# Expert gathers of a PEER block: second choice and first Gelu moved, V rows and dense V spread differently

## What is computed

```python
q = (hf @ w_q).reshape(n_tok, 8, 2, 128)                       # 8 heads, two half queries
half_scores = einsum('thpd,hpnd->thpn', q, sub_keys)           # 128 keys in each half
s_top, i_top = top_k(half_scores, 16)
cand = s_top[:, :, 0, :, None] + s_top[:, :, 1, None, :]       # 16 x 16 pairs
best, pos = top_k(cand, 16); expert_idx = take(i0 * 128 + i1, pos); gates = softmax(best)
act = einsum('td,thkd->thk', xb, u_tab[ib])                    # 16384 experts, rows of 2048
w = gates * gelu(act)
out = einsum('thk,thkd->td', w, v_tab[ib])
x = layer_norm(alpha * x + (1 + gate2) * out)
```

## Time and profile before

| | us |
|---|---|
| median of 3 runs (2278.86 to 2285.75) | 2281.61 |
| the profiled execution, its own time | 2278.52 |
| its span, from first to last instruction | 2276.9 |
| PE busy, share of the span | 1937.7, 85% |
| DVE busy | 1365.1, 60% |
| POOL busy | 782.8, 34% |
| ACT busy | 390.6, 17% |
| all of DMA: 722.41 MB, mean | 317 GB/s |

### The profile page before, as it was taken

How to read it: one execution, slowest core, us unless ns; L and a number is a source line. 1 busy time by engine, 2 the same in 40 slices (tenths; PEclk the granted TensorE clock), 3 DMA queues, 4 the chain that set the end, 5 groups by cost and what they waited for, 6 DMA issues and landing times.

```text
span 2276.9 us, 27806 instructions
## 1 busy us (share of the span) xinstructions
PE 1937.7 (85%) x10646; PEld 1309.3 (58%) x10646; DVE 1365.1 (60%) x2008; ACT 390.6 (17%) x1001; POOL 782.8 (34%) x554
## 2 busy tenths in 40 slices
PE   4899899998999999989888888888975888897455
PEld 4788688887888888878654545555640222221001
DVE  7821378776444441246798889777876444444664
ACT  0112212211000001021232212544530000000011
POOL 1000000000000000004365546767878644554783
PEclk9999899999999999999899899888985999999556
DMA  9963366575576656318899999999999999999997
GB/s 391 428 276 143 116 270 246 216 292 197 234 284 245 230 212 259 140 69 331 311 383 414 405 408 414 398 402 398 392 406 371 417 417 410 399 413 354 364 365 270
DMA packets 104603, 722.41 MB, mean 317 GB/s; under 512 B 29740, under 2 KB 29740, under 8 KB 32060
## 3 DMA queue, kind: packets, MB, share of 16 engines
q0 software_dynamic: 78800, 466.66, 51.9%
q1 hardware_dynamic: 25696, 254.35, 28.0%
HBM read 858.35 MB, written 4.19 MB: 379 GB/s over the span
## 4 chain that ended last, share of the span: by engine, by line
PE 43%; DMA 29%; DVE 12%; issue 8%; POOL 5%; ACT 2%; POOLq 0%; DVEq 0%; SPq 0%; ACTq 0%
PE ps L777 21%; DMA arena<-expert_u,expert 14%; DMA arena<-expert_v,expert_q 11%; PE ps L785 10%; POOL arena L489 4%; PE ps L801 3%; PE ps L974 3%; DVE work L1410 2%; PE ps L1002 2%; DMA mod_rows<-expert_u,expert 2%; DVE mod_rows L1167 1%; PE ps L1048 1%; DMA mod_rows<-expert_v,expert_q 1%; DVE work L1223 1%; DVE work L1130 1%
## 5 line engine op out<-in xcount | busy, mean ns | idle before, releaser
L1410 DVE CUSTOM_DVE_ANT_0 work<-arena,buf_b 128x2048 f32<-128x2048 f32 x166 | 380.8, 2294 | 265.5 <-DMA arena<-expert_u,expert 232.1
L974 PE MATMUL ps<-arena,mod_rows 128*32 128x512 f32 x1640 | 270.5, 740 | 197.1 <-DMA arena<-expert_v,expert_q 166.0
L777 PE MATMUL ps<-buf_a,arena 128*128 128x256 f32 x1920 | 424.2, 383 | 6.1 <-DVE arena L1241 5.3
L777 PEld LDWEIGHTS ps<-buf_a,arena 128*128 128x128 f32 x1920 | 367.5, 192 | 57.2 <-issue 6.7
L489 POOL DMA_INDIRECT arena<-expert_v,expert_q x205 | 339.8, 1658 | 159.1 <-PE ps L974 97.1
L489 POOL DMA_INDIRECT arena<-expert_u,expert x205 | 266.1, 1298 | 239.8 <-DVE work L1410 124.2
L476 POOL DMA_DIRECT2D arena<-ada_late x32 | 16.9, 529 | 770.9 <-DVE mod_rows L1167 642.7
L1002 PE MATMUL ps<-arena 128*128 128x256 f32 x1024 | 273.3, 418 | 4.2 <-DMA arena<-dense_u 4.2
L1002 PEld LDWEIGHTS ps<-arena 128*128 128x128 f32 x1024 | 202.8, 207 | 128.8 <-issue 94.8
L974 PEld LDWEIGHTS ps<-arena,mod_rows 128*32 128x32 f32 x1640 | 37.2, 118 | 333.2 <-DMA arena<-expert_v,expert_q 270.3
L653 ACT ACTIVATE work<-work 32x4 f32<-32x4 f32 (+3 forms) x320 | 66.4, 207 | 551.3 <-DVE work L1410 543.8
(11 more groups left out here) (244 smaller groups left out, 2083.1 us busy)
## 6 DMA issues: line engine op xcount, KB each, us to landing
arena<-weights SPq DMA_DIRECT2D x62, 2048.0 KB, 8.0
arena<-ada_late POOLq DMA_DIRECT2D x32, 2048.0 KB, 9.4
arena<-ada_early SPq DMA_DIRECT2D x16, 2048.0 KB, 17.7
arena<-dense_u SPq DMA_DIRECT2D x32, 1024.0 KB
arena<-expert_v SPq DMA_DIRECT2D x32, 1024.0 KB
arena<-w_early SPq DMA_DIRECT2D x8, 1536.0 KB, 9.8
arena<-expert_u,expert POOLq DMA_INDIRECT x205
arena<-expert_v,expert_q POOLq DMA_INDIRECT x205
```

The costliest lines, as they stand in the source:

```text
L777: last = mm(ps[:, bank, c * TOKENS:(c + 1) * TOKENS], ring[slot][:, first + k, c * P:(c + 1) * P], rhs[:, k, :], start=(k == 0), stop=(k = ...
L974: last = mm(ps[j * GROUP:(j + 1) * GROUP, n // HEADS * QUADS + g, :], spread_w[n % 2][:, e, :], v_slot[row % V_RING][:, j * QCOLS:(j + 1) ...
L1410: v.tensor_tensor_reduce(out=products[n > 2], in0=u_slot[s], in1=h2[:, n // HEADS], scale=1.0, scalar=0.0, op0=ALU.mult, op1=ALU.add, accu ...
```

## The change

It moves work within the fixed orders of the PEER stage; no operation is added or left out in what is computed.

- The second choice is made beside the rows (0, 1), (0, 3), (0, 5), (0, 7).
- ACT: `soft_exp(1)` stands at projection 3, and `gates_to_quads(0)` with `gelu(0)` at projection 5 (all three stood at projection 4).
- PE: the last two projections are cut into eight groups of matmuls each, with a V row of head 0 after each, so all 16 V(0) rows are done there. The loop for n = 1 then has no V rows.
- POOL: V(0, 5) to V(0, 15) are issued beside U(1, 4) to U(1, 10), one or two to a step.
- The pieces of the first 20 dense U tiles are spread over (1, 0) to (4, 15) (before: (1, 9) to (4, 15)). `GELU_AT` follows from it.
- The pieces of dense V are spread over the 81 steps (9, 13) to (14, 13) (before: the 64 steps (10, 0) to (13, 15)).
- Block 0's rows are added from (15, 4) on, every second row, and finished behind the last U row; means, variances and rstd move accordingly, and two table preloads of ACT in head 15 go.

```diff
@@ -355,17 +355,18 @@
         F_END = tuple(n + m * 4 for n, m in zip(F_QUERY, (1, 1, 0, 0)))
 
         FIRST_MASKS = 5
-        FIRST_BESIDE = 8
         row_order = [(n, e) for n in range(BLOCKS * HEADS) for e in range(TOPK)]
-        choice_steps = row_order[2:TOPK:4] + [row_order[TOPK + i * 64 // 56] for i in range(56)]
-        dense_steps = [row_order[TOPK + FIRST_BESIDE + 1:5 * TOPK], row_order[5 * TOPK:9 * TOPK - 4]]
+        choice_steps = row_order[1:TOPK // 2:2] + [row_order[TOPK + i * 64 // 56] for i in range(56)]
+        dense_steps = [row_order[TOPK:5 * TOPK], row_order[5 * TOPK:9 * TOPK - 4]]
         mask_steps = [(n, e) for n in range(FIRST_MASKS, HEADS + 1) for e in range(TOPK)]
-        v_steps = [(n, e) for n in range(HEADS + 2, HEADS + 6) for e in range(TOPK)]
+        v_steps = row_order[10 * TOPK - 3:15 * TOPK - 2]
 
         def shares(steps, count):
 
             return {step: range(i * count // len(steps), (i + 1) * count // len(steps)) for i, step in enumerate(steps)}
 
+        LATER_V0 = {e: range(V_RING + first, V_RING + end) for e, first, end in
+                    ((4, 0, 2), (5, 2, 3), (6, 3, 5), (7, 5, 6), (8, 6, 8), (9, 8, 9), (10, 9, 11))}
         BEFORE_MASKS = 20
         DENSE_U_AT = shares(dense_steps[0], 4 * BEFORE_MASKS)
         for step, pieces in shares(dense_steps[1], 4 * (DENSE - BEFORE_MASKS)).items():
@@ -517,8 +518,9 @@
                         wait_alone(pool, s_exq, (2, 5, HEADS + 1).index(n) + 2)
                     if n > 1:
                         gather_v(n - 1, e)
-                    elif V_RING <= e + 1 < TOPK:
-                        gather_v(0, e + 1)
+                    else:
+                        for later in LATER_V0.get(e, ()):
+                            gather_v(0, later)
             for e in range(TOPK):
                 gather_v(BLOCKS * HEADS - 1, e)
 
@@ -732,8 +734,9 @@
                     soft_exp(0)
                 if h == 1:
                     experts_to_quads(0)
-                if h == 4:
+                if h == 3:
                     soft_exp(1)
+                if h == 5:
                     gates_to_quads(0)
                     gelu(0)
                 if h == 6:
@@ -755,12 +758,9 @@
                     for t in TOKENS_AT.get((n, e), ()):
                         if t % 2 == 0:
                             mask_cols(t)
-                    if n == BLOCKS * HEADS - 1 and e == 6:
-                        nc.scalar.preload_act_table_set("natural_log_exp_and_others")
-                        rstd_of_groups(0, 0, QUADS)
-                        nc.scalar.preload_act_table_set("gelu_and_others")
                 gelu(n)
             nc.scalar.preload_act_table_set("natural_log_exp_and_others")
+            rstd_of_groups(0, 0, QUADS)
             for g in range(QUADS):
                 rstd_of_groups(1 + g, QUADS + g, QUADS + g + 1)
 
@@ -1043,16 +1043,16 @@
             for h in range(HEADS):
                 s = h % 2
                 pe.wait_ge(loaded[s], (F_QUERY[s] + h // 2 + 1) * 16)
-                for i in range(4):
-                    for k in range(8 * (i % 2), 8 * (i % 2) + 8):
-                        last = mm(ps[:, 6 + s, i // 2 * TOKENS:(i // 2 + 1) * TOKENS], ring[s][:, k, i // 2 * P:(i // 2 + 1) * P],
+                for i in range(8):
+                    for k in range(4 * (i % 4), 4 * (i % 4) + 4):
+                        last = mm(ps[:, 6 + s, i // 4 * TOKENS:(i // 4 + 1) * TOKENS], ring[s][:, k, i // 4 * P:(i // 4 + 1) * P],
                                   h2_t[:, k, :], start=k == 0, stop=k == KT - 1)
-                    if i == 3:
+                    if i == 7:
                         last.then_inc(used[s], 1)
                     if h == HEADS - 2 and i == 0:
                         pe.wait_ge(s_wgt, 1)
                     if h >= HEADS - 2:
-                        weigh_row(0, 4 * (h - HEADS + 2) + i)
+                        weigh_row(0, 8 * (h - HEADS + 2) + i)
                 pe.wait_ge(s_pq, h + 1)
                 if h > 1:
                     pe.wait_ge(s_kept, h - 1)
@@ -1071,17 +1071,18 @@
                     pe.wait_ge(s_slot, BLOCKS)
                 if n == HEADS + 1:
                     pe.wait_ge(s_dw, BATCHES)
-                for e in range(FIRST_BESIDE if n == 1 else 0, TOPK):
-                    weigh_row(n - 1, e)
+                for e in range(TOPK):
+                    if n > 1:
+                        weigh_row(n - 1, e)
                     for i in DENSE_U_AT.get((n, e), ()):
                         dense_u_piece(i)
                     for t in TOKENS_AT.get((n, e), ()):
                         spread_gates(t)
                     for i in DENSE_V_AT.get((n, e), ()):
                         dense_v_piece(i)
-                    if n == BLOCKS * HEADS - 2 and e == 13:
+                    if n == BLOCKS * HEADS - 1 and e == 13:
                         means(0, range(QUADS))
-                    if n == BLOCKS * HEADS - 1 and e == 4:
+                    if n == BLOCKS * HEADS and e == 1:
                         variances(0, range(QUADS))
                     if n == BLOCKS * HEADS and e >= QUADS and e % QUADS == 1:
                         means(e // QUADS, [QUADS + e // QUADS - 1])
@@ -1544,7 +1545,7 @@
                         weigh_dense(WEIGH_AT[n, e])
                     for a in MIXED_AT.get((n, e), ()):
                         mix(a)
-                    if (n, e) >= (BLOCKS * HEADS - 2, 4) and e % 2 == 0:
+                    if n == BLOCKS * HEADS - 1 and e >= 4 and e % 2 == 0:
                         next(block0, None)
                 if n == FIRST_MASKS - 1:
                     for _ in picks:
```

## The result

The changed kernel takes **2295.92 us** (median of 7 runs, 2288.59 to 2299.25), the kernel before 2281.85 us in the same comparison (2278.86 to 2285.83, 7 runs): ratio **1.0050**, 95% interval 1.0039 to 1.0061. The forecast was 2279 with a range of 2264 to 2293; the change makes the kernel 14.1 us slower by the medians, 11.4 by the ratio. The profiled execution took 2299.25 us, its span is 2297.6 us. Its first U row, (0, 0), starts 2.9 us later than in the profile before (1044.27 against 1041.42), in a stage that the change does not touch. A lag comes from one profile of each kernel, so it shows where time is lost better than how much: the last row's is 17.3 us where the medians differ by 14.1.

The account below looks back on a forecast made before the run. The prediction took DMA bytes, at about 410 GB/s, to bound the stage. Its terms, +2 for the start, -6.5 for dense V and +2 for the end, gave -2.5 us: about 2279 us by the median, range 2264 to 2293.

Parts of the forecast that it names:

- Part 1: Start, up to row (1, 10): earlier choice and copy bring weights and row (1, 1) 5.4 us earlier, at 1112.7.
- part 2: Row (1, 10): DVE waits 16 us (12 to 18) for soft_exp(3) behind the first dense Gelu; row (2, 1) 11 us late.
- parts 1 to 3: Start to head 5: 11 us late, less 6.4 and 2.6 won back, sums to +2 us (-4 to +8).
- What bounds the stage: PEER stage from 1000 us: bytes bound it; time is lost only where DMA's rate falls below about 410 GB/s.
- The end of the projections: Last projection matmul on PE, with 16 V rows in two projections: 1157.3 us, where it was 1151.7.
- POOL's pace: Gathers during the last projections: 2.08 us each, 18 take 37 us, until 1150; V rows land just in time.
- Part 3: Rows (2, 1) to (5, 0): 6.4 us won back by earlier dense pieces and 2.6 (0 to 6) by full slots.
- sign set for row (5, 0): Row (5, 0) starts within 4 us of 1420.48 + 2; a start before 1414 would refute the stall or its recovery.
- slow rival: Rows (2, 1) to (5, 0) stay at 4.85 us, so the stall is kept: +10, 2292 us; chance 0.18.
- Part 4: Dense V over 81 steps: 17 gathers-only steps become mixed at 0.41 us each; -6.5 us (-8 to +1).
- Part 5: The end: block 0's stores meet the last V gathers; +2 us (0 to +7).
- The rivals: Stall repaid in full, 2269, chance 0.30; stall kept, 2292, 0.18; dense V's spreading wins nothing, 2286, 0.10.

Follow-up runs that it names:

- e14: Kernel before with the second choice at (0, 1) to (0, 7) and the first Gelu behind projection 5, nothing else: 2286.58 us, ratio 1.0014.
- e1: Kernel before with the change's parts up to head 5 alone (choice, Gelu, V(0) rows, dense U from (1, 0)): 2295.47 us, ratio 1.0048.
- e3: Changed kernel with the Gelus of dense tiles 0 to 4 moved behind the exponential: 2295.05 us, ratio 1.0044 to the kernel before.
- e4: Changed kernel with dense U put back to start at (1, 9): 2286.12 us, ratio 1.0006 to the kernel before.
- e9: Kernel before with dense U pieces from step (1, 0) on and nothing else of the change: 2298.48 us, ratio 1.0067.
- e2: Kernel before with dense V over (9, 13) to (14, 13) and block 0 finished at the end alone: 2285.54 us, ratio 1.0001.
- e6: Kernel before with dense V over (9, 0) to (13, 15), some early products left out of the output: 2279.05 us, ratio 0.9971.
- e10: Kernel before with dense V over (9, 0) to (13, 15), first write to each bank opening it, product complete: 2278.08 us, ratio 0.9981.
- e5: e2 with SyncE's reload of x moved up behind the ninth dense V tile: 2285.60 us, ratio 1.0002 to the kernel before.
- e13: Kernel before with block 0's adds and finish at the end and nothing else: 2285.17 us, ratio 1.0011.
- e7: Kernel before with the reload of x done twice, one behind the other: 2305.65 us, ratio 1.0094.
- e11: Kernel before with the reload of x in 32 transfers of 64 KB, partition quarters in turn: 2281.72 us, ratio 0.9984.

## Why the prediction was wrong, point by point

Three steps failed. Part 1's lead of 5.4 us at row (1, 1) did not come (it was -0.5), and the time at which TensorE and ScalarE reach the first dense tile, from which part 2's lag of 11 us is worked out, was 14 us too early, so the lag was 23.5. And part 2 saw the queue of dense tiles on TensorE ahead of the first V(1) row, but put no cost on it. The sum of parts 1 to 3 was +2 and measured +11.4.

**What bounds the stage** was read rightly. The chain by line from 1000 us on still has U and V landings first, and the loss of the start stands in the windows as holes in the rate.

**Part 1 failed: "Weights and row (1, 1) come 5.4 us earlier".** Row (1, 1) came 0.5 us later than before, the first V row 0.4. I took the choice's 15.7 us wait as what held row (1, 0), since POOL named it. But what DVE waited for was data. From 1080 to 1115 us of the profile after, the DMA queues (packets, MB, share of 16 engines) moved

```profile
q0 software_dynamic: 1892, 9.77, 68.3%
q1 hardware_dynamic: 340, 4.78, 32.2%
```

that is gathers on q0 and the projections' weights on q1, at 416 GB/s together. An earlier request joined a full queue, with more gathers of the same stretch beside it; e14 has the same. On ACT I moved the copy in front of the Gelu but left out that `gates_to_quads(0)` (3.62 us) and the table load (1.28) move along with it; the Gelu ended at 1114.23, 1111.4 without the offset. This slip was not what failed: of the 4 us from the end of row (1, 0) to row (1, 1) only 0.9 are the weights, which need the Gelu, and 3.1 are a piece of a choice, which does not. With the data there the weights could have been done near 1112.3, an estimate from these durations. e14 tested this part by itself: no gain.

**The end of the projections** came at 1170.23, 1167.4 without the offset, where I had 1157.3. Of these 10.1 us, 5.7 are the late first V row. Of the 4.4 behind it, 2.2 are TensorE's clock, which the text took as full: the engine had stood for 14.67 us, the granted clock from 1121 to 1125 was 0.50, the 1.2 GHz level, and the first V row and the group behind it took 1.93 and 3.29 us where later ones took 1.07 and 1.99. Another 1.6 us are two V rows that landed late. **POOL's pace** was priced rightly: its 17 gathers from 1124.27 on went out at 2.08 us each.

**A wait that the text does not have.** The lag was 0.5 us at row (1, 5) and 4.1 at (1, 6). Between them VectorE waits 3.68 us in `normed_gates` for `soft_exp(2)`, which ScalarE runs behind projection 6; with eight V rows in it in place of four, that projection ends at 1144.1, 1141.2 without the offset, where it ended at 1132.3. The step at (1, 6) stands in e1, e3 and e4 as well (lags of 3.9, 4.1 and 3.6 us), and not in e9 and e14, which have four V rows there (-0.1 and 0.1). With 1.0 us more of waiting for data, row (1, 10) was 5.1 us behind before, where the forecast had it 5.4 ahead.

By the Trainium skill ("SBUF — State Buffer", Who interferes with whom) the reductions would not hold a gather up. The trace after disagrees as the one before did: a gather issued at 1090.34, during a reduction that began at 1089.54, lasted 2.36 us, others in the same stretch 0.99. But a gather also reads its indices from SBUF, and for GpSimd's reads the page does expect contention; no run here tells the two apart.

**Part 2: the wait was there, where and why the text said**, 19.9 us for the 16 (12 to 18) forecast, with the table load and the exponential right behind the first dense Gelu. What was wrong is the time of day. The exponential ran at 1190.55, 1187.7 without the offset, against 1173.8: 13.9 us late. That is 10.1 from the end of the projections, 2.2 for the landing (9.15 us from issue, I took 7 where the row before had 8.9), and 2.0 for the four pieces, which took 9.47 us where I had 2 x 3.72, less 0.4 of roundings. The pieces have their reason in a row that I had before me: TensorE stood 7.14 us and its granted clock from 1179 to 1183 was 0.50, the 1.2 GHz level; the eight that took 3.28 us in the earlier trace rows had run at a granted clock of 0.66 (1160 to 1164), behind an idle stretch of 4.22 us. DVE reached the wait about 10 us later than forecast and stood 4 us longer, so row (2, 1) was not 11 but 23.5 us late.

**The second queue.** The text says "PE's five tiles of n = 1, at 8 us each, end at 1204 too, so the first V(1) row comes then" and does nothing with it. That is a second wait of the same size, seen and costed at nothing; in the changed kernel it lay in the first one's shadow, and e3 brought it to light.

**Part 3 held in size.** From (2, 1) to (5, 0) the lag fell from 23.5 to 15.3, so 8.2 us were won back for the 9.0 forecast, and 10.1 by (8, 0). The sign set for row (5, 0), within 4 us of 1422.5, failed by what came before it: it started at 1435.8 without the offset. The slow rival's condition, rows of over 4.7 us, did not come: (2, 1) to (5, 0) took 219.8 us for 47 rows, 4.68. Its time, 2292, was the nearest of the four, for another reason: not slow rows, but a lag twice as long to begin with. Parts 1 to 3 came to +11.4 (e1) in place of +2, outside their bounds of -4 to +8: 9.4 of the miss of 16.9. (By the text's own terms, a lag of 7 to 13 less 6.4 and less 0 to 6, the bounds are -5.4 to +6.6.) Parts 4 and 5 are another 4.7 to 6.0, by e2.

**Part 4 was over-sized in its place.** The price of 0.41 us a step is what e6 and e10 measured where the added steps are in head 9, but I put it on 17 steps in all, 14 of them in head 14, and there little came that these runs can tell from nothing. The bounds held it (-8 to +1). From (9, 13) until the reload was issued at 2139 the rate was 408 GB/s as forecast, but before had 411 over its own stretch of dense V, from 1748 to 2072; then it fell to 298 from 2140 to 2200, with the reload in it. From row (8, 12) to the last U row the profile after took 3.8 us longer, where the text had 6 to 7 less. Why the spread to the end wins so little stays open: the reload's place is not it (e5), block 0's finish is 2 us of it (e13), and no run here has the spread to head 14 with block 0's finish where it was. By the Trainium skill ("DMA: Bandwidth & Descriptors", Where 436 GB/s comes from) 358 GB/s would bind with a pair of cores streaming; one core alone ran at 394 to 419 in 15 of the 16 slices from 1206 to 2125, so that rule is not what ate this term.

**Part 5 held.** From the last reduction to the end 52.9 us passed, 52.3 before; the first group of block 1 is added at 2262.22, 17.5 us behind the last reduction, 13.2 before. VectorE's four finishes waited 4.1 us for ScalarE, of which at most 0.6 reached the end. e13 measured +1.6 to +2.5 for the +2.

**The chances.** 0.22 stood on slower, and the range ended 3 us short. The rivals all shared part 1's lead of 5.4 us, and none had the queue on TensorE, so that the range had no case in which it did not come.

## What to carry to other kernels

A wait that names a late instruction is a gain only if nothing else ends at the same place: before an earlier request is credited, look whether the queue that serves it is full. Work moved to earlier steps of an in-order program does not run earlier than its input, here the slot freed by the last projection; it piles up there, and everything behind it on every engine that holds a part of it (here TensorE's V rows, ScalarE's exponentials, the head's Gelu) has to be gone through, since taking away the longest of several such waits alone brings nothing. A step's price holds for the stretch it was read in, so an edit is best tried where the row stands.

## What the runs showed of the hardware

- Loading 2 MB a second time, in pieces of 2 KB into 32 partitions a transfer, costs 20.4 us of the kernel's time (e7), though at 410 GB/s the bytes are 5.1 us; interleaving the partitions of the one reload wins 2.8 to 3.7 us (e11). With a reload under way DMA's share stands at 1.02 to 1.03 while it moves only 309 to 321 GB/s.
- A gather (some 0.77 MB by the rate of the earlier trace rows, 369 x 100 / 48) issued while DMA's share was 1.01 landed after 21 us, one issued into the hole of before after 6.9 (1104.99 to 1111.88 in the profile before).
- TensorE's granted clock was 0.50 (1.2 GHz) after 14.67 us and after 7.14 us of waiting; a V row then took 1.93 us for 1.07, a group of eight matmuls 3.29 for 1.99.
- A single profiled execution lies up to 5 us from the median of its kernel's runs (2290.41 against 2285.54 in e2), as much as most terms argued over here. The costs of the experiments are from medians and ratios; waits, lags and the split of parts 1 and 2 are from one profile of each kernel.
